# Attention in a two-model kernel: ScalarE's exponentials issued two steps ahead of its copies of the transposed weights, in place of one

## What is computed

```python
s = jnp.einsum('cbhqd,cbhkd->cbhqk', qb, k) * scale
p = _masked_softmax(s, mask)          # exp(s - max) / sum
a = p[0] - lam_full * p[1]            # differential attention only
return jnp.einsum('bhqk,bhkv->bhqv', a.astype(v.dtype), v)
```

## Time and profile before

| | us |
|---|---|
| median of three timed runs | 2703.06 |
| lowest and highest of them | 2702.91, 2707.96 |
| the profiled execution | 2708.64 |
| its span, first to last instruction | 2706.7 |
| PE busy | 2327.9 |
| DVE busy | 565.2 |
| ACT busy | 376.9 |
| stage a0 (first scores to last output) | 138 to 192 |
| stage a1 | 623 to 711 |
| mix0, mix1 | 1151 to 1206, 1697 to 1755 |

### The profile page before, as it was taken

One profiled execution on the slowest core, in us unless ns is written; L12 is line 12 of the kernel. 1 busy time (PEld: TensorE's weight loads), 2 busy tenths in 40 slices (PEclk: granted clock), 3 DMA queues, 4 the chain that ended last, 5 costly groups with the idle time before them and its releaser, 6 DMA issues. The chain is left out here.

```text
span 2706.7 us, 39272 instructions
## 1 busy us (share of the span) xinstructions
PE 2327.9 (86%) x16254; PEld 1566.4 (58%) x16254; DVE 565.2 (21%) x1856; ACT 376.9 (14%) x1106; POOL 143.5 (5%) x191
## 2 busy tenths in 40 slices
PE   6978776799977678869799999688899999999997
PEld 4836333485653336647688887467656555555544
DVE  1143311225441113032200020321311011111112
ACT  2031110105321001130100001311000000000001
POOL 0000000000000000820000007200000000000000
PEclk9988888887978889969899999588899999999998
DMA  9482999955359996202334433022579769799995
GB/s 379 181 349 98 401 422 422 372 199 210 123 220 421 422 422 263 109 1 81 122 124 156 163 129 112 1 78 94 202 297 365 301 263 349 281 421 422 422 422 219
DMA packets 95031, 679.14 MB, mean 251 GB/s; under 512 B 10624, under 2 KB 11313, under 8 KB 13361
## 3 DMA queue, kind: packets, MB, share of 16 engines
q1 hardware_dynamic: 94897, 677.18, 62.6%
HBM read 676.09 MB, written 1.05 MB: 250 GB/s over the span
## 5 line engine op out<-in xcount | busy, mean ns | idle before, releaser
L543 PE MATMUL B<-W,BIG 128*32 128x128 f32 (+3 forms) x7488 | 671.3, 413 | 145.8 <-DMA W<-in_wf 93.0
L543 PEld LDWEIGHTS B<-W,BIG 128*32 128x32 f32 (+2 forms) x7488 | 364.6, 125 | 437.1 <-issue 238.7
L543 PE MATMUL B<-H,W 128*128 128x256 f32 x1888 | 416.4, 383 | 15.5 <-DVE H L1564 10.8
L543 PEld LDWEIGHTS B<-H,W 128*128 128x128 f32 x1888 | 361.6, 192 | 68.8 <-issue 11.5
L543 PE MATMUL B<-BIG 128*128 128x128 f32 (+5 forms) x1792 | 289.5, 356 | 62.4 <-DVE ATT L1655 25.5
L543 PEld LDWEIGHTS B<-BIG 128*128 128x128 f32 (+2 forms) x1792 | 214.9, 204 | 155.5 <-issue 60.4
L543 PE MATMUL B<-W,ATT 128*32 128x256 f32 (+1 forms) x1408 | 213.4, 495 | 0.0
L543 PE MATMUL B<-BIG,W 128*128 128x256 f32 x768 | 184.1, 402 | 19.8 <-DVE BIG L1564 8.6
L543 PEld LDWEIGHTS B<-BIG,W 128*128 128x128 f32 x768 | 155.4, 203 | 48.7 <-DVE BIG L1564 9.4
L1964 DVE COPY BIG<-B 128x384 f32<-128x384 f32 (+1 forms) x88 | 43.2, 491 | 595.6 <-PE B L543 583.4
L543 PEld LDWEIGHTS B<-W,ATT 128*32 128x32 f32 (+1 forms) x1408 | 61.4, 122 | 110.9 <-issue 102.5
(11 more groups left out here) (284 smaller groups left out, 1460.7 us busy)
## 6 DMA issues: line engine op xcount, KB each, us to landing
W<-in_wf SPq DMA_DIRECT2D x513, 1024.0 KB, 16.6
W<-in_wa SPq DMA_DIRECT2D x75, 1024.0 KB, 6.9
W<-in_ada SPq DMA_DIRECT2D x48, 1024.0 KB, 8.4
W<-in_xo SPq DMA_DIRECT2D x8, 512.0 KB, 3.5
CON<-in_consts SPq DMA_DIRECT2D x1, 1410.5 KB, 6.3
BIG<-in_x SPq DMA_DIRECT2D x1, 1024.0 KB, 6.1
BIG<-in_mem SPq DMA_DIRECT2D x1, 1024.0 KB, 24.9
out<-BIG SPq DMA_DIRECT2D x1, 1024.0 KB, 4.0
```

Source lines behind the costliest of these rows:

```text
L543: return nc.tensor.matmul(out, lhsT, rhs, start=start, stop=stop, **kw)
```

## The change

In ScalarE's `attend`, exps(1) is issued right behind exps(0), and in each step exps(p+2) stands where exps(p+1) stood: ahead of the ada copy, of transposed(p) and of outputs(p-1). The set of instructions is the same, and no other engine's order changes. No buffer is added: front(p+2), for which exps(p+2) waits, stands behind back(p) on VectorE, so the two places for maxima and sums and the three for weights are free by then.

```diff
                 exps(0)
+                exps(1)
                 for p in range(len(pairs)):
-                    if p + 1 < len(pairs):
-                        exps(p + 1)
+                    if p + 2 < len(pairs):
+                        exps(p + 2)
                     for i in ada_ended(tag, p):
                         ada_copy(i)
                     transposed(p)
```

## The result

The changed kernel takes 2716.78 us (median of five runs, 2711.92 to 2718.78) beside 2703.06 for the kernel before: 1.0042 of its time, with a 95% interval of 1.0029 to 1.0055. It is slower, by 13.7 us where I had forecast 4.3, and above the range that I gave. The profiled execution is the one of 2718.78 us, 10.1 above that of before.

What follows compares the result with a forecast made beforehand. TensorE was taken as the bound, ScalarE's order mattering only where TensorE waits for it. Terms -1.2 + 3.8 + 1.5 + 0.2 = +4.3 us on the 2703.06 median gave 2707.4 us (+0.16%), range 2701.5 to 2713.

Steps and rivals of the forecast that it cites:

- a0, -1.2: End of a0: exps(7) runs in ScalarE's idle time, so turn(7) starts earlier; gain 1.2 us.
- a1 with units, 0, step 8 0.1 to 0.3: a1 steps with adaLN units: TensorE work covers the later copy, cost 0; step 8, without a unit, 0.1 to 0.3 us.
- Order in a1's tail, +2.6: a1 steps 17 to 22: 3.00 us per step against 2.59; with step 8, a cost of 2.6 us.
- The loop: a1's tail: dependency chain over two steps, from turn(q-1) through exps(q+2) and transposed(q) to turn(q+1); 6.82 us for long pairs.
- Clock in a1, +1.2 on the guess that it falls at the same time: a1's tail: clock still falls at about 702.7, so more of the delayed work runs slowly; cost 1.2 us.
- rival B: a1's tail: looser TensorE loses its clock 3 to 10 us earlier; +8 us, 2711 us in all, chance 0.27.
- mix0, +1.5: End of mix0: exps(5) goes ahead of transposed(3), delaying the chain behind it; cost 1.5 us.
- mix1, +0.2: End of mix1: same place at low clock, transposed(3) starts 0.23 us late; cost 0.2 us.
- I let all of it go through to the end: Linear layers behind each stage: weights are not late, so the whole +4.3 us sum reaches the kernel's end.
- Rival C: Copies not on the path, ScalarE's wait covered by other work: -1 to +2 us, 2703.5 us, chance 0.20.
- Rival D: a1's tail: earlier exponentials remove waits before mix and keep the clock up; -5 us, chance 0.08.

Runs made afterwards that it cites:

- after: The changed kernel itself, exponentials two steps ahead in every stage, against the kernel before: 2716.78 us, ratio 1.0042.
- a0_only: Kernel before with exponentials two steps ahead in stage a0 alone, one step elsewhere: 2703.61 us, ratio 0.9996.
- a1_fill1: Kernel before with two steps ahead in a1 alone, plus one unused matmul ahead of mix in a1's steps 18 to 23: 2709.27 us, ratio 1.0020.
- mix_last: Changed kernel with only the last exponentials, exps(5), of mix0 and mix1 put back to their old place: 2708.59 us, ratio 1.0029.
- a1_only: Kernel before with exponentials two steps ahead in a1 alone: 2721.56 us, ratio 1.0052.
- by_units: Kernel before with exponentials two steps ahead only in steps that carry an adaLN unit: 2702.51 us, ratio 0.9994.
- wait_only: Kernel before, old order, but transposed(p) also waits for front(p+2): 2705.97 us, ratio 1.0006.
- late_mix0: Kernel before with four unused matmuls added behind the last mix of mix0: 2707.09 us, ratio 1.0011.
- a1_look: Second run of the kernel before with two steps ahead in a1 alone: 2718.37 us, ratio 1.0048.
- mix_only: Kernel before with exponentials two steps ahead in mix0 and mix1 alone: 2711.63 us, ratio 1.0029.
- warm_mix: Kernel before with two steps ahead only in adaLN-unit steps, plus unused matmuls in TensorE's waits ahead of mix work, none in tails: 2705.52 us, ratio 0.9992.
- warm_more: Kernel before with two steps ahead only in adaLN-unit steps, plus unused matmuls in the mixes' waits and tails and ahead of a1's first scores: 2702.66 us, ratio 1.0003.

## Why the prediction was wrong, point by point

- **a0, -1.2: right.** turn(6) to turn(7) 3.10 to 1.89 us, in after and a0_only. That it reaches the end isn't shown, being below what a0_only can tell.
- **a1 with units, 0, step 8 0.1 to 0.3: a little low.** +0.5 in after to turn(16). From turn(5) to turn(16), at full clock, it is 34.8 us in each profile with the old order and 35.3 in each with the new.
- **Order in a1's tail, +2.6: nearly right**, 2.5 by a1_fill1 and 2.2 by mix_last. The loop is there too: at full clock the six steps from turn(16) took 18.20 us in mix_last, 3.03 each where I had said 3.00, and 15.99 before, 2.67 each where I had said 2.59.
- **Clock in a1, +1.2 on the guess that it falls at the same time: this step failed.** It fell ahead of turn(19), and the seven steps held 9.0 us of low clock. Against a profile without any it costs 3.2 to 3.5; the profile of before had itself 3.9 us of it, which made it a poor zero. That was my rival B, mechanism and place (a fall before 700). I gave it +8 in all and it is +13.7.
- **mix0, +1.5: right in the term, wrong in the sum.** The order is worth 1.4 at full clock. But the stage took 3.4 more, since the clock rose a pair later. a1_only has that without the order.
- **mix1, +0.2: right**, +0.1. The clock is low there in both.
- **"I let all of it go through to the end": this failed as well.** I asked of the linear layers behind a stage only whether their weights are late. They have a clock too. 4.0 us came up behind mix0 and 0.9 behind a1, in code that is the same, and no term of mine stood for it.
- **Rival C** (the copies are not on the path) is refuted by a1_only, +0.52% (0.33 to 0.71). The Trainium skill ("Perfetto Trace Analysis", Identifying the Most-Contended Engine) says of the engine with the highest occupancy "Optimize this engine first." That is TensorE here, 86% busy; ScalarE is 14% busy, and its order in one stage alone costs half a per cent. **Rival D** found nothing: no tail became denser.

By terms: order -1.2 + 0.5 + 2.5 + 1.4 + 0.1 = 3.3 us, or 3.0 with 2.2 for a1's tail. The other 10 are a remainder that I put down to the clock; the two profiles show 8.7 us of it (1.9 in a1's tail, 2.0 in mix0, 3.9 and 0.9 behind the two), less 2.1 won behind a0. A rougher reading gives the clock less. Over the 109 runs of the kernel before, 0.001 of mean granted clock goes with 1.2 us of time. At equal clock, by that slope, the changed kernel is some 7 us slower, so by this way the clock's part is about half. Between half and three quarters is what I can say.

**Open.** The chain is shown only in part: where mix0 has the old order, a tail of a1 with no low clock or 4 us of it goes with a mix0 of 27.0 to 27.1 us in every profile (before, a0_only, by_units, wait_only, a1_fill1, late_mix0), and one with 9 us of it with 30.3 or 30.4 (a1_only, a1_look). But how an event at 700 us decides where the clock rises at 1195 isn't shown. mix_only has its 29.73, by its own order, without it, and warm_mix, which has the old order there and some unused matmuls ahead of it, has 30.33 behind a tail of a1 with no low clock. So the link is two profiles against six, and a third cause of both isn't excluded. Nor is it settled why mix_last's a1 kept its clock, or what brings the 4.0 us behind mix0.

## What to carry to other kernels

Price an order on a lightly loaded engine by its consumer. If a group that waits is put ahead of a copy that is ready, the cost is less the wait (0.3 us in seven steps) than that the group itself then runs first: 1.4 us for a group of 1.8 in mix0, 0.3 to 0.4 a step in a1's tail. Under other work it is nearly free, 0.5 us in the steps of a1 with units. And where the consumer is TensorE, add a term for its clock, for the stage and for what follows: look where the granted clock changes in the profile of before, and take any loosening ahead of such a place as a risk of several times the term itself. Take more than one profile of before as the zero, since the place can differ by a few us between two.

## What the runs showed of the hardware

- A full engine at the low clock. TensorE was busy for 14.98 of 15.00 us in mix0 and the granted clock stayed at 0.50, 1.2 GHz, while in the loose end of mix0, 8.54 of 12 us, it held 0.98. The Trainium skill ("TensorE: Matmul & The Clock Gate", Part 1) says that "activity releases the throttle". By the busy time of the profile that doesn't hold here. The matmuls of that stretch are small ones, scores on 64 rows and biases on 8; that this is the reason isn't shown.
- One filling matmul per step, 0.45 us, kept the clock at 1.00 in a tail that otherwise lost 3.2 to 3.5 us to it; TensorE had 10.46 of 11.70 us busy there for 9.20.
- The places at which the clock changes come back to the same few matmuls (four of four in a1, over two kernels), and a change of 4.0 us recurs in unchanged code, in the same three pieces, while eight other profiles have none of it. That made it countable. It is not strict: the a1 of mix_last is the same code with the clock risen 10 us earlier and then kept.
- TensorE stood still for 5.4 to 7.3 us at two places behind 2100 us in seventeen profiles, with no releaser in the profile, and for 12.6 and 12.3 us in the one of warm_more.
